# A two-block transformer kernel: the first stage rebuilt, four stalls of TensorE reordered, and every SBUF tile moved to a multiple of 512 bytes

## The chip, the cores and the metric

The kernel is one program on one NeuronCore of a Trainium2 chip. The metric is the device time of one execution in microseconds. TensorE (PE) multiplies, VectorE (DVE), ScalarE (ACT) and GpSimd (POOL) do the element-wise work, and SyncE (SP) issues nearly all transfers. All data are fp32 in memory; a product is made of three fp32r products of "high" and "low" parts.

## What is computed

Two transformer blocks on x of 512 tokens x 1024 features. Only what the change touches is shown:

```python
def rmsnorm(x, g):
    y = x32 * lax.rsqrt(jnp.mean(jnp.square(x32), axis=-1, keepdims=True) + EPS)
    return (y * g).astype(x.dtype)

# block 1
h = rmsnorm(x, norm_mix_g)
q, k, v, xr, gr, g_attn, g_rnn = split(h @ w_in)          # 8 heads of 128 columns each in q, k, v
attn_out = diff_attention(rmsnorm(q), rmsnorm(k), v, rel_bias, lam)
r = sigmoid(conv(xr) @ w_a + b_a); i = sigmoid(conv(xr) @ w_x + b_x)
a = exp(-8 * r * softplus(-lru_lambda));  hidden = scan(a, sqrt(1 - a*a) * i * conv(xr)) * gelu(gr)
x = x + (sigmoid(g_attn) * (attn_out @ w_proj_attn) + sigmoid(g_rnn) * (hidden @ w_proj_rnn)) @ w_out
x = x + square(relu(rmsnorm(x) @ w_up)) @ w_down
# block 2: short convolution, forgetting attention, window attention, a merge of the three with gates,
# cross attention to a memory of 256 tokens, a gated feed-forward layer, a last rmsnorm
```

## The kernel before

Activations are kept transposed, features on the partitions and the 512 tokens along the free axis. A matrix product goes by **units**: one unit is 128 output columns over all of its input, 8 tiles of 128 x 128 weights, 24 matmuls of 128 x 512. For each unit SP loads the weights into one of four slots of RAW (L417), GpSimd cuts them into WH (L597) and WL (L600) after a tiny operation on `gate` (L596), TensorE makes hi x hi, lo x hi and hi x lo into the slot's PSUM bank (L630, L632, L634), and VectorE takes the bank (L1540 and others), mostly times RSTD. The input is HH and HL, the two parts of x times the norm's gain; RSTD, the reciprocal root of the mean square of each token, is applied when a bank is taken, so it isn't needed before that. The list PHASES gives the order of the units; each engine has its own program, and semaphores order them. A unit may start when its weights are cut (`unit_cut`), and the bank's last contents are taken (`taken`).

**First stage.** SP loads the gain, both halves of x, 17 small rows of parameters, three units of weights and ten small tables. TensorE transposes x into two banks in turn (L671), ScalarE copies each into X (L1104), makes HH (L1063) and the square (L1065), VectorE makes HL (L1453) from X and HH and adds the squares into ACC0 (L1458). Between them VectorE takes the transposed parameters and the rows of the bias table (BROW, L1524). Then ones x ACC0 gives the sums (L661), ScalarE the root (L1069), VectorE the reciprocal over 128 x 512 (L1463). TensorE runs the three units of head 0; VectorE takes q and k, then computes softplus(-lru_lambda) by a chain of 24 dependent operations on 128 x 8 (L1591 to L1603), and only then scales q and k (L1549), cuts them, takes v and the attention's constants (L1612). Head 0's scores (L748) wait for all this.

**Attention, 8 heads.** `attend` weaves the 72 matmuls of the next head's three units into the 8 score groups, the transposes (L714) and the value products (L725) of this head, by a `share`. At a head's end a root (L1074, L1075) scales the output (L1641), which is cut into AO (L1645); only after that VectorE begins the next head's row maxima (L1572).

**Recurrent stage, 8 rounds.** Each is `rnn_gates(n)` (L825 to L827), which needs the cut convolution XCH, XCL of VectorE (L1667), and four units. **Merge.** `merge1` has two units a round, one from HH, one from the recurrent output RO, all eight tiles of which the first round waits for. Block 2's merge starts with YC (L928), the convolution's output, and YF.

**Layout.** Tiles lie one behind the other in the order of their `sb(...)` calls; `push` and `pop` reuse memory.

Of the kernel before, what the change touches and what calls it, by code (L numbers as in the profile page):

```python
# [173 lines left out]
def program(nc, x, out, w, causal_rows, window_rows):  # L174

    units = Units()
    with ExitStack() as top:
# [11 lines left out]
        class Sems(dict):  # L189
# [10 lines left out]
            "vector_step": ["tab_masked", "gain_taken", "par_taken", "brow_rows", "decay_abs", "lam_dots", "lam_row", "lam_taken",  # L200
# [3 lines left out]
            "tensor_step": ["gain_done", "par_done", "brow_done", "lam_done", "forget_placed", "mem_stat"],  # L204
# [10 lines left out]
        def norm_event(tag, kind, n):  # L215


            k = int(tag[1]) - 1
# [20 lines left out]
        SUM, NMAX, RS = sb("SUM", [P, 8]), sb("NMAX", [P, 8]), sb("RS", [P, 8])  # L239
        column, n = {}, 0  # L240
# [20 lines left out]

        SQ1, ACC1, STD1 = sb("SQ1", [P, 2, S]), sb("ACC1", [P, S]), sb("STD1", [P, S])

# [5 lines left out]
        SQ0 = sb("SQ0", [P, 2, S])  # L269
        ACC0, STD0 = sb("ACC0", [P, S]), sb("STD0", [P, S])  # L270
        VROWS = sb("VROWS", [P, 2, P])
        ONEHOT = sb("ONEHOT", [BUCKETS + 1, BIAS1_W + BIAS2_W])
        TAB = sb("TAB", [BUCKETS + 1, 2, HEADS])
        BROW = sb("BROW", [HEADS, BIAS1_W + BIAS2_W])
# [3 lines left out]
        LOGT = sb("LOGT", [P, 8, 8])  # L278
# [8 lines left out]
        def attention_memory(tag, parts, cols):  # L287
# [12 lines left out]
            if tag == "a":  # L300
# [9 lines left out]
        XR = sb("XR", [P, S + 3])  # L310
# [4 lines left out]
        MG = sb("MG", [P, DC, S])  # L315
        GA, SG, GT, G2 = SQ1[:, 0, :], SQ1[:, 1, :], ACC1, STD1
# [20 lines left out]
        push()  # L337
        FLEFT = sb("FLEFT", [P, S], F32R)
        FRIGHT = ACC1[:]
        FROW = sb("FROW", [P, 2, S], F32R)  # L340
        pop()
        CB, CC, CV = SQ1[:, 0, :], SQ1[:, 1, :], ACC1[:]
        ZP = sb("ZP", [P, S + 2])
# [32 lines left out]
        ACC, STD, SQS = ({tag: first if tag == "n1" else later for tag in GAIN}  # L376
                         for first, later in ((ACC0, ACC1), (STD0, STD1), (SQ0, SQ1)))

# [31 lines left out]
        def _(sp):  # L410
# [15 lines left out]
            for half in range(2):  # L426
# [21 lines left out]
            for j in range(3):  # L448
                load("qkv", 0, j, cols(w["w_in"], D * j))
            sp.dma_start(ONEHOT[:, 0:BIAS1_W], causal_rows).then_inc(S_["tab_landed"], 16)  # L450
            sp.dma_start(ONEHOT[:, BIAS1_W:], window_rows).then_inc(S_["tab_landed"], 16)
            sp.dma_start(TAB[0:BUCKETS, 0, :], w["rel_bias"]).then_inc(S_["tab_landed"], 16)
            sp.dma_start(TAB[0:BUCKETS, 1, :], w["rel_bias_2"]).then_inc(S_["tab_landed"], 16)
            for k, name in enumerate(("lambda_q1", "lambda_k1", "lambda_q2", "lambda_k2")):
                sp.dma_start(LAM[:, k, :], w[name].rearrange("(o c) -> o c", o=1)).then_inc(S_["lam_landed"], 16)
            sp.dma_start(small[0:HEADS, FBIAS:FBIAS + 1], w["forget_bias_2"].rearrange("(p o) -> p o", o=1)
                         ).then_inc(S_["lam_landed"], 16)
            sp.dma_start(SROW[:, 0:8], w["sink_2"].rearrange("(o c) -> o c", o=1)).then_inc(S_["lam_landed"], 16)

# [5 lines left out]
            for h in range(1, HEADS):  # L465
# [92 lines left out]
        def _(pool):  # L558
            nc.gpsimd.memset(ident[:], 0.0).then_inc(once("ident_clear")[0], 1)
# [1583 lines left out]
```

## Time and profile before

| | us |
|---|---|
| median of 3 runs (lowest, highest) | 2112.77 (2111.72, 2116.9) |
| the profiled execution: its own time | 2114.88 |
| its span, first to last instruction | 2113.1 |
| TensorE busy in it | 1979.3 |
| until the first score of head 0 | 58.54 |
| one attention head in the steady state | 31.40 |
| recurrent stage, from 318.0 to 503.5 | 185.5 |

The span is what the rows are counted in. Busy times of TensorE overlap (a 128 x 512 matmul is shown as 0.39 us, and the next begins 0.23 us after it), so idle time is read from the waits and the starts, not from the busy share.

### The profile page before, as it was taken

Reading aid. Unit: us, or ns where it says so; the run is one execution under the profiler, and the core shown is the slowest. Engines: PE = TensorE matmul, PEld = TensorE weight load, DVE = VectorE, ACT = ScalarE, POOL = GpSimd, SP = SyncE. Lnnn points to the kernel's source line nnn. Section 1 sums busy time; section 2 is a strip of 40 time slices with the busy share of each in tenths; the row PEclk is TensorE's granted clock in tenths of the full one; section 3 lists DMA queues with packets and bytes.
Section 4 is the critical chain, followed back from the end, with each engine's and each line's share of the span. In section 5 each row is a group of like instructions: output and inputs, shape, how many; then the busy total and the mean of one; then the engine's idle time right before and its main releaser. Section 6 shows DMA issues by size and latency. Waiting matters only on the chain.

```text
span 2113.1 us, 23477 instructions
## 1 busy us (share of the span) xinstructions
PE 1979.3 (94%) x9015; PEld 1608.9 (76%) x9015; DVE 1071.6 (51%) x1522; ACT 501.7 (24%) x1001; POOL 1232.1 (58%) x1014
## 2 busy tenths in 40 slices
PE   6888869999999999999799988999989899999997
PEld 4666658887888888888587777888778778888886
DVE  7666658996364132237765664333455463223134
ACT  4444433432122011022233322101222221001012
POOL 6233327777767676666233433677767567667662
PEclk8999989999999999999899989999999999999999
DMA  5122112333333333333112311333433323333321
GB/s 155 46 68 62 47 33 77 105 94 94 95 95 95 93 97 97 92 100 90 50 51 60 70 55 45 100 92 98 120 100 90 90 82 99 94 95 100 90 85 55
DMA packets 341169, 177.39 MB, mean 84 GB/s; under 512 B 14453, under 2 KB 338203, under 8 KB 341060
## 3 DMA queue, kind: packets, MB, share of 16 engines
q1 hardware_dynamic: 339044, 173.28, 28.4%
q10 hardware_dynamic: 2016, 2.62, 0.6%
q8 instruction: 73, 1.20, 0.2%
q14 instruction: 36, 0.29, 0.0%
HBM read 173.75 MB, written 2.13 MB: 83 GB/s over the span
## 4 chain that ended last, share of the span: by engine, by line
PE 75%; DVE 18%; ACT 3%; issue 3%; DMA 0%; ACTq 0%; DVEq 0%; SPq 0%
PE bank L630 22%; PE bank L634 22%; PE bank L632 22%; PE bank L748 2%; PE bank L725 1%; DVE aPR L1580 1%; PE bank L696 1%; DVE aPR L1582 1%; DVE aPR L1572 1%; PE bank L714 1%; DVE HS L1691 1%; DVE IT L1680 1%; DVE ACC L1685 1%; DVE XC L1661 1%; DVE HS L1690 1%
## 5 line engine op out<-in xcount | busy, mean ns | idle before, releaser
L600 POOL TENSOR_TENSOR WL<-RAW,WH 128x1024 fp32r<-128x1024 f32 (+3 forms) x331 | 814.3, 2460 | 27.6
L630 PE MATMUL bank<-HH,WH 128*128 128x512 f32 x1560 | 623.6, 400 | 2.3 <-DVE HL L1453 2.3
L634 PE MATMUL bank<-HH,WL 128*128 128x512 f32 x1560 | 619.0, 397 | 0.0
L632 PE MATMUL bank<-HL,WH 128*128 128x512 f32 x1560 | 616.2, 395 | 0.0
L596 POOL TENSOR_TENSOR gate<-gate 128x1 f32<-128x1 f32 x331 | 81.6, 246 | 822.0 <-PE bank L634 770.9
L630 PEld LDWEIGHTS bank<-HH,WH 128*128 128x128 f32 x1560 | 296.9, 190 | 67.1 <-issue 6.9
L597 POOL TENSOR_SCALAR WH<-RAW 128x1024 fp32r<-128x1024 f32 (+3 forms) x331 | 343.2, 1037 | 0.9 <-issue 0.2
L632 PEld LDWEIGHTS bank<-HL,WH 128*128 128x128 f32 x1560 | 296.4, 190 | 60.8 <-issue 3.1
L634 PEld LDWEIGHTS bank<-HH,WL 128*128 128x128 f32 x1560 | 295.8, 190 | 60.9 <-issue 1.7
L1731 DVE TENSOR_TENSOR X<-X,bank 128x512 f32<-128x512 f32 x80 | 54.9, 686 | 210.6 <-PE bank L634 210.6
L1453 DVE SCALAR_TENSOR_TENSOR HL<-X,PARAM,HH 128x512 fp32r<-128x512 f32 x40 | 89.1, 2226 | 30.3 <-ACT HH L1063 30.3
L630 PE MATMUL bank<-UH,WH 128*128 128x512 f32 x256 | 101.5, 397 | 0.0
L634 PE MATMUL bank<-UH,WL 128*128 128x512 f32 x256 | 101.2, 395 | 0.0
L632 PE MATMUL bank<-UL,WH 128*128 128x512 f32 x256 | 101.2, 395 | 0.0
L1235 ACT ACTIVATE SU<-TU 128x512 f32<-128x512 f32 x32 | 20.3, 636 | 263.5 <-DVE TU L1750 263.4
L1750 DVE SCALAR_TENSOR_TENSOR TU<-bank,RSTD 128x512 f32<-128x512 f32 x32 | 22.1, 692 | 115.5 <-PE bank L634 115.5
L630 PE MATMUL bank<-FFH,WH 128*128 128x512 f32 x176 | 70.3, 399 | 0.6 <-DVE FFL L2067 0.6
L632 PE MATMUL bank<-FFL,WH 128*128 128x512 f32 x176 | 69.6, 395 | 0.0
L634 PE MATMUL bank<-FFH,WL 128*128 128x512 f32 x176 | 69.6, 395 | 0.0
L1540 DVE TENSOR_TENSOR GA<-bank,RSTD 128x512 f32<-128x512 f32 x24 | 16.6, 692 | 102.8 <-PE bank L634 102.8
L1063 ACT ACTIVATE HH<-X,PARAM 128x512 fp32r<-128x512 f32 x40 | 28.9, 723 | 128.5 <-DVE X L1731 128.5
L630 PEld LDWEIGHTS bank<-UH,WH 128*128 128x128 f32 x256 | 48.1, 188 | 12.8 <-issue 1.4
(399 smaller groups left out, 3210.1 us busy)
## 6 DMA issues: line engine op xcount, KB each, us to landing
RAW<-in_w_in SPq DMA_DIRECT2D x107, 512.0 KB, 3.7
RAW<-in_w_up SPq DMA_DIRECT2D x32, 512.0 KB, 4.0
RAW<-in_w_down SPq DMA_DIRECT2D x32, 512.0 KB, 3.9
RAW<-in_w_ffn_gate SPq DMA_DIRECT2D x22, 512.0 KB, 3.7
RAW<-in_w_ffn_up SPq DMA_DIRECT2D x22, 512.0 KB, 3.8
RAW<-in_w_xkv SPq DMA_DIRECT2D x16, 512.0 KB, 3.8
RAW<-in_w_ffn_down SPq DMA_DIRECT2D x16, 512.0 KB, 3.5
RAW<-in_w_proj_attn SPq DMA_DIRECT2D x8, 512.0 KB, 3.9
```

What stands on the lines that cost most here:

```text
L596: nc.gpsimd.tensor_tensor(gate[:, 1:2], gate[:, 0:1], gate[:, 0:1], ALU.add)
L597: nc.gpsimd.tensor_scalar(WH[:, s, 0:k, :], RAW[:, s, 0:k, :], 1.0, 1.0, ALU.mult, ALU.mult).then_inc(S_[f"hi_made{s}"], 1)
L600: nc.gpsimd.tensor_tensor(WL[:, s, 0:k, :], RAW[:, s, 0:k, :], WH[:, s, 0:k, :].bitcast(F32), ALU.subtract).then_inc(S_[f"unit_cut{s}"], 1)
L630: mm(psum[s][:, 0:n], WH[:, s, k, :], hi(k), start=(k == 0), stop=False)
L632: mm(psum[s][:, 0:n], WH[:, s, k, :], lo(k), start=False, stop=False)
L634: last = mm(psum[s][:, 0:n], WL[:, s, k, :], hi(k), start=False, stop=(k == tiles - 1))
L696: mm(STAT[:], lhs, rhs, start=True, stop=True).then_inc(S_[tag + "_stat"], 1)
L748: last = mm(bank, M[q][:, part, i * P:(i + 1) * P], M[k][:, 2, k0:k1], start=(q == "QH" and k == "QH"), stop=(q == "QL" and not add_bias), ...
L1063: A(HH[:, bass.ds(e, 1), :], x_e, ACT.Copy, scale=par(GAIN[tag], e)).then_inc(norm_event(tag, "hh", 0)[0], 1)
L1453: V.scalar_tensor_tensor(HL[:, bass.ds(e, 1), :], X[:, bass.ds(e, 1), :], par(GAIN[tag], e), HH[:, bass.ds(e, 1), :].bitcast(F32), ALU.mul ...
L1731: take(name, it, j, lambda bank: V.tensor_tensor(x_e, x_e, bank[:].unsqueeze(1), ALU.add))
L1750: take("mlp", g, j, lambda bank: V.scalar_tensor_tensor(TU[:, j % 2, :], bank[:], 0.0, RSTD[:], ALU.max, ALU.mult))
```

## The change

- **Loads.** SP loads weights and x in turn: unit 0, first half of x, unit 1, second half, unit 2, then the rows of parameters, and the three units of head 1. The ten small tables and vectors go to ScalarE's queue.
- **x.** Transposes go to four banks. ScalarE makes HH and VectorE HL straight from the bank (one operand in PSUM); VectorE also copies the bank into X, for the last four tiles after all of HL. The sums of squares are made by ScalarE over the tokens (four squares of 128 x 1024 with a running sum, 128 x 1 each); root and reciprocal are on 128 x 4; four diagonal blocks (DIAG) and one matmul with ones spread them into RSTD.
- **Order.** TensorE weaves the transposes, q's and k's products, runs 9 matmuls of v, then the statistic, the bias rows, the rest of v, the parameters, and then the 24 matmuls of head 1's q before head 0's attention; head 0's `share` weaves in the 48 that are left.
- **Decay chain.** The 24 operations are made 5 at a time in heads 1 to 5, between the take of v and the wait for the root.
- **Waits.** `rnn_gates(0)` is run after the next two units; `merge1` waits for RO tile by tile; the merge of block 2 starts with YF and waits for YC tile by tile; `f_out_taken` 9 is asked only before YS.
- **Tiles.** pad_low (96 elements) ahead of X, LOGT and pad_small (16) into the small tiles, XR to the end of its group, ZP (514 wide) replaced by CZ, which lies in STD1, with the taps of the convolution written as shifted ranges; FROW, FLEFT and FRIGHT move to the place of SQ1, ACC1 and STD1.

```diff
@@ layout
+        sb("pad_low", [P, 96])
         X = sb("X", [P, DC, S])
...
         SUM, NMAX, RS = sb("SUM", [P, 8]), sb("NMAX", [P, 8]), sb("RS", [P, 8])
+        LOGT = sb("LOGT", [P, 8, 8])
+        sb("pad_small", [P, 16])
...
+        push()
+        FROW, FLEFT = sb("FROW", [P, 2, S], F32R), sb("FLEFT", [P, S], F32R)
+        pop()
         SQ1, ACC1, STD1 = sb("SQ1", [P, 2, S]), sb("ACC1", [P, S]), sb("STD1", [P, S])
+        FRIGHT = STD1[:]
...
-        XR = sb("XR", [P, S + 3])
         XC = sb("XC", [P, S])
...
         MG = sb("MG", [P, DC, S])
+        XR = sb("XR", [P, S + 3])
...
-        ZP = sb("ZP", [P, S + 2])
...
+        XBANK = [WORK[0], WORK[1], psum[2], psum[3]]
+        X_LATE = (6, 7, 4, 5)
@@ sync
+            load("qkv", 0, 0, cols(w["w_in"], 0))
+            load_x(0)
+            load("qkv", 0, 1, cols(w["w_in"], D))
+            load_x(1)
+            load("qkv", 0, 2, cols(w["w_in"], D * 2))
...
             for j in range(3):
-                load("qkv", 0, j, cols(w["w_in"], D * j))
...
+                load("qkv", 1, j, cols(w["w_in"], P + D * j))
             sp.wait_ge(*once("brow_rows"))
             sp.dma_start(scr, BROW[:]).then_inc(S_["brow_stored"], 16)
@@ gpsimd
-            clear_queries("a", M1, M1["OR"][:])
...
                 cut(name, it, j)
+                if (name, it, j) == ("qkv", 0, 2):
+                    clear_queries("a", M1, M1["OR"][:])
@@ tensor
+            def x_transposed(e):
...
+                if e >= 4:
+                    pe.wait_ge(S_["n1_x"], e - 3)
                 for t in range(NB):
-                    last = nc.tensor.transpose(WORK[e % 2][:, t * P:(t + 1) * P], XTOK[:, t, e * P:(e + 1) * P],
+                    last = nc.tensor.transpose(XBANK[e % 4][:, t * P:(t + 1) * P], XTOK[:, t, e * P:(e + 1) * P],
                                                ident[:])
...
+            for e in range(4):
+                x_transposed(e)
+            queries0, keys0 = from_h("qkv", 0, 0, cut_of("n1")), from_h("qkv", 0, 1)
+            for e in range(DC):
+                run(queries0, 3)
+                if e < 4:
+                    x_transposed(e + 4)
+                if e >= 3:
+                    run(keys0, 3)
+            run(keys0)
+            pe.wait_ge(S_["n1_x"], 5)
+            values0 = from_h("qkv", 0, 2)
+            run(values0, 9)
+            pe.wait_ge(S_["n1_diag"], NB)
+            mm(STAT[:], ones[:], DIAG[:], start=True, stop=True).then_inc(norm_event("n1", "stat", 0)[0], 1)
+            bias_rows()
+            run(values0)
+            parameters()
             pe.wait_ge(*norm_event("n1", "std", 1))
...
+            steps0 = chain(*[from_h("qkv", 1, j) for j in range(3)])
             for side in range(2):
-                run(values0, 9)
+                run(steps0, 6)
                 qk_stat1(0, 0, side)
-            run(values0)
+            run(steps0, 6)
...
+            run(steps0, 6)
             pe.wait_ge(*once("lam_taken"))
+            pe.wait_ge(*once("brow_rows"))
 
             def head1(h, last):
+                if h == 0:
+                    steps, share = steps0, (3, 8, 8, 2)
...
             for n in range(DC):
-                rnn_gates(n)
+                if n:
+                    rnn_gates(n)
...
                 if n == 0:
+                    rnn_gates(0)
...
+                run(from_pair("merge1", e, 1, RO, cut_pair("ro_hi", "ro_lo") if e == 0 else None))
...
-            pe.wait_ge(S_["yc_lo"], 4)
-            pe.wait_ge(S_["f_out_taken"], 9)
+            pe.wait_ge(S_["f_out_taken"], 5)
...
-                for k in range(8):
+                for k in (4, 5, 6, 7, 0, 1, 2, 3):
@@ scalar
+            for e in range(DC):
+                act.wait_ge(S_["xt_done"], e + 1)
+                A(HH[:, e, :], XBANK[e % 4][:], ACT.Copy, scale=par(GAIN["n1"], e)
+                  ).then_inc(norm_event("n1", "hh", 0)[0], 1)
...
+                if e in (3, 4, 5, 7):
+                    token_squares({3: 0, 4: 1, 5: 2, 7: 3}[e])
+            act.wait_ge(S_["n1_ssq"], NB)
+            A(SSQ[:], SSQ[:], ACT.Sqrt, bias=EPSC[:], scale=1.0 / D).then_inc(S_["n1_root"], 1)
@@ vector
             for e in range(DC):
-                norm_chunk("n1", e, e % 2)
...
+                V.scalar_tensor_tensor(HL[:, e, :], XBANK[e % 4][:], par(GAIN["n1"], e), HH[:, e, :].bitcast(F32),
+                                       ALU.mult, ALU.subtract).then_inc(norm_event("n1", "hl", 0)[0], 1)
+                if e < 4:
+                    x_copy(e)
+            for e in X_LATE:
+                x_copy(e)
...
+            own.link(V.reciprocal(SSQ[:], SSQ[:]))
+            for t in range(NB):
+                V.tensor_scalar(DIAG[:, t * P:(t + 1) * P], ident[:], SSQ[:, t:t + 1], None, ALU.mult
+                                ).then_inc(S_["n1_diag"], 1)
+            dve.wait_ge(*norm_event("n1", "stat", 1))
+            V.tensor_copy(RSTD[:], STAT[:]).then_inc(norm_event("n1", "std", 0)[0], 1)
...
             take_qk1(0, 0)
+            take_qk1(0, 1)
+            bias_rows()
+            parameters()
...
                     take("qkv", h + 1, 2, scaled(M1["VR"][:]))
+                for _step in range(5 if 0 < h else 0):
+                    next(decays, None)
```

## Rows read from the trace of the kernel before

**Rows 1.** The page's totals by engine.

```profile
PE 1979.3 (94%) x9015; PEld 1608.9 (76%) x9015; DVE 1071.6 (51%) x1522; ACT 501.7 (24%) x1001; POOL 1232.1 (58%) x1014
```

**Rows 2.** Table of stretches: start:end, length, busy us of each engine, clock, DMA.

```profile
0.00:58.54 58.54, 34.75 (x121) 23.52 (x122) 47.40 (x84) 24.45 (x39) 31.84 (x37) 0.80 0.52 148
58.54:90.06 31.52, 28.97 (x129) 22.82 (x129) 19.04 (x42) 13.24 (x31) 8.38 (x8) 0.93 0.14 43
90.06:121.46 31.40, 27.58 (x130) 20.93 (x129) 20.87 (x44) 14.97 (x34) 11.09 (x10) 1.00 0.20 59
318.00:503.50 185.50, 180.78 (x787) 147.56 (x787) 168.09 (x135) 70.39 (x94) 145.35 (x117) 1.00 0.33 95
```

**Rows 3.** The waits of PE over the span: total us, times, longest.

```profile
PE bank L748 <- DVE small L1612: 11.7, 1, 11.7
...
PE bank L825 <- DVE XCL L1667: 9.4, 1, 9.4
...
PE bank L928 <- DVE YCL L1922: 1.8, 1, 1.8
```

**Rows 4.** Timeline, 0 to 58 us: start, us, engine, line, what.

```profile
6.33 1.94 PE L671 MATMUL bank<-ident,XTOK 128*128 128x128 f32 x8 [6.33 <-DMA XTOK<-in_x]
...
10.04 0.71 ACT L1063 ACTIVATE HH<-X,PARAM 128x512 fp32r<-128x512 f32 x1
...
10.87 0.75 DVE L1453 SCALAR_TENSOR_TENSOR HL<-X,PARAM,HH 128x512 fp32r<-128x512 f32 x1 [2.12 <-ACT HH L1063]
...
13.13 0.68 POOL L596 TENSOR_TENSOR gate<-gate 128x1 f32<-128x1 f32 x1 [7.27 <-DMA RAW<-in_w_in]
...
15.28 2.83 DVE L1458 TENSOR_TENSOR ACC<-ACC,SQ 128x512 f32<-128x512 f32 x1
...
32.77 1.02 PE L661 MATMUL bank<-ACC,ones 128*128 128x512 f32 x2
...
34.62 3.35 DVE L1463 RECIPROCAL RSTD<-STD 128x512 f32<-128x512 f32 x1 [1.58 <-ACT STD L1069]
...
42.13 2.21 DVE L1593 TENSOR_TENSOR LOGT<-LOGT 128x8 f32<-128x8 f32 x1
...
44.38 0.17 DVE L1594 TENSOR_TENSOR LOGT<-LOGT 128x8 f32<-128x8 f32 x1
```

**Rows 5.** What the DMA engines moved, 0 to 60 us in 40 slices of 1.5 us.

```profile
GB/s 0 15 393 400 399 238 202 271 312 272 82 3 0 0 0 0 0 0 0 22 46 210 244 333 291 303 266 77 302 41 178 172 57 288 5 233 117 0 0 0
```

**Rows 6.** Timeline, 482 us: a PSUM-sourced VectorE instruction beside a GpSimd one.

```profile
482.29 2.72 POOL L600 TENSOR_TENSOR WL<-RAW,WH 128x1024 fp32r<-128x1024 f32 x1
...
482.67 0.68 DVE L1698 SCALAR_TENSOR_TENSOR MG<-SQ,bank 128x512 f32<-128x512 f32 x1
```

**Rows 7.** Timeline, 120 to 127 us: the seam between attention heads 1 and 2.

```profile
120.73 1.05 POOL L597 TENSOR_SCALAR WH<-RAW 128x1024 fp32r<-128x1024 f32 x1
...
121.86 2.39 POOL L600 TENSOR_TENSOR WL<-RAW,WH 128x1024 fp32r<-128x1024 f32 x1
...
123.45 1.35 DVE L1641 SCALAR_TENSOR_TENSOR aOR<-aOR,small,aRQ 128x512 f32<-128x512 f32 x1 [2.29 <-ACT aRQ L1075]
...
126.53 0.39 PE L748 MATMUL bank<-aQH 128*128 128x256 f32 x1 [1.08 <-DVE NMAX L1572]
```

**Rows 8.** Timeline of the recurrent stage: two waits of DVE, and PE's at its end.

```profile
324.26 0.69 DVE L1656 TENSOR_TENSOR XR<-bank,RSTD 128x512 f32<-128x512 f32 x1 [1.55 <-PE bank L634]
...
347.63 0.69 DVE L1656 TENSOR_TENSOR XR<-bank,RSTD 128x512 f32<-128x512 f32 x1 [1.71 <-PE bank L634]
...
503.52 0.77 PE L630 MATMUL bank<-ROH,WH 128*128 128x512 f32 x1 [4.75 <-issue]
```

**Rows 9.** PE's timeline: first matmuls of 384 on HH/HL, of 192 on FFH/FFL, and the next.

```profile
1865.14 0.39 PE L630 MATMUL bank<-HH,WH 128*128 128x512 f32 x1
...
1952.23 0.39 PE L630 MATMUL bank<-FFH,WH 128*128 128x512 f32 x1
...
1997.20 0.39 PE L630 MATMUL bank<-HH,WH 128*128 128x512 f32 x1
```

More of the change, by code:

```diff
@@ L375, in program @@
                 "n5": "ffn_norm_g_2", "n6": "final_norm_g_2"}
-        ACC, STD, SQS = ({tag: first if tag == "n1" else later for tag in GAIN}
-                         for first, later in ((ACC0, ACC1), (STD0, STD1), (SQ0, SQ1)))
+        ACC, STD, SQS = ({tag: tile for tag in GAIN if tag != "n1"} for tile in (ACC1, STD1, SQ1))
+        XBANK = [WORK[0], WORK[1], psum[2], psum[3]]
+        X_LATE = (6, 7, 4, 5)
         scr = nc.dram_tensor("bias_rows", [HEADS, BIAS1_W + BIAS2_W], F32).ap()
@@ L425, in _, with load_x @@
             sp.dma_start(VROWS[0:r, 0, :], w[name].rearrange("(r c) -> r c", c=P)).then_inc(S_["gain_landed"], 16)
-            for half in range(2):
+            def load_x(half):
                 sp.dma_start(XTOK[:, :, half * S:(half + 1) * S],
@@ L464, in _ @@
                 sp.dma_start(BIAS1[:, h, :], toeplitz_of(h, 0)).then_inc(S_[f"bias_landed{h}"], 16)
-            for h in range(1, HEADS):
+            for h in range(2, HEADS):
                 for j in range(3):
@@ L558, in _ @@
         def _(pool):
+            for s in range(SLOTS):
+                pool.sem_inc(S_[f"unit_cut{s}"], 1)
+                pool.sem_inc(S_[f"hi_made{s}"], 1)
             nc.gpsimd.memset(ident[:], 0.0).then_inc(once("ident_clear")[0], 1)
@@ L688, in _, with parameters @@
-            mm(psum[2][0:8, 128:512], TAB[:, 1, :], ONEHOT[:, 640:1024], start=True, stop=True
-               ).then_inc(once("brow_done")[0], 1)
+            def parameters():
+                pe.wait_ge(S_["rows_landed"], 16 * N_ROW_LOADS)
+                pe.wait_ge(*once("gain_taken"))
+                na, nb = sum(r for _, r in ROWS_A), sum(r for _, r in ROWS_B) + 2
+                nc.tensor.transpose(OUTB[:, 0:na], VROWS[0:na, 0, :], ident[0:na, 0:na])
+                nc.tensor.transpose(OUTB[:, 96:96 + nb], VROWS[0:nb, 1, :], ident[0:nb, 0:nb]
+                                    ).then_inc(once("par_done")[0], 1)
@@ L795, in _ @@
             pe.wait_ge(S_["lam_landed"], 96)
-            mm(psum[3][:, 0:16], ones[0:1, :], SROW[0:1, 0:16], start=True, stop=True).then_inc(once("lam_done")[0], 1)
+            pe.wait_ge(*once("par_taken"))
+            mm(OUTB[:, 160:176], ones[0:1, :], SROW[0:1, 0:16], start=True, stop=True).then_inc(once("lam_done")[0], 1)
+            run(steps0, 6)
             pe.wait_ge(*once("lam_taken"))
+            pe.wait_ge(*once("brow_rows"))
             def head1(h, last):
-                steps = chain(from_h("first", 0, 0), from_h("first", 0, 1)) if last else \
-                    chain(*[from_h("qkv", h + 1, j) for j in range(3)])
-                attend("a", M1, KIND1, h, steps, (2, 8, 8, 3) if last else (5, 10, 10, 2),
+                if h == 0:
+                    steps, share = steps0, (3, 8, 8, 2)
+                elif last:
+                    steps, share = chain(from_h("first", 0, 0), from_h("first", 0, 1)), (2, 8, 8, 3)
+                else:
+                    steps, share = chain(*[from_h("qkv", h + 1, j) for j in range(3)]), (5, 10, 10, 2)
+                attend("a", M1, KIND1, h, steps, share,
@@ L843, in _ @@
                     run(from_h("rnn", n, 4))
-            for e in range(DC):
-                run(from_h("merge1", e, 0))
-                if e == 0:
-                    pe.wait_ge(S_["ro_hi"], DC)
-                    pe.wait_ge(S_["ro_lo"], DC)
-                run(from_pair("merge1", e, 1, RO))
             def cut_pair(hi, lo, base=0):
@@ L1143, in _ @@
             qk_hi1(0, 1)
+            act.wait_ge(*once("decay_abs"))
+            A(LOGT[:, 1, :], LOGT[:, 0, :], ACT.Exp, scale=-1.0).then_inc(once("decay_exp")[0], 1)
             def head1(h, last):
@@ L1905, in conv2 @@
                 if n == 3:
-                    take(*conv_unit(h, last, 2), scaled(ZP[:, 2:]))
+                    take(*conv_unit(h, last, 2), scaled(CZ))
                 if n == 4:
```

196 lines of the change are left out of this document (91 added, 105 removed).

## The prediction

> **What bounds the kernel now.** I read the page's totals first: TensorE is busy 94% of the span [rows 1], so a change is worth what it takes from TensorE's idle time or from the spacing of its matmuls. The list of its waits says where it idles [rows 3]: 11.7 us before head 0's first score, 9.4 us before the first `rnn_gates`, 1.8 us before the merge of block 2. A wait of 4.75 us before the first product from RO is seen in the timeline alone [rows 8]. The table of stretches [rows 2] shows the largest loss: head 0's attention begins at 58.54 us, with 72 product matmuls done, which take 3 x 5.44 = 16.3 us at the later spacing [rows 9], and TensorE's clock is 0.80 of full on average there. VectorE is busy 47.4 of these 58.5 us: the first stage is bound by VectorE, and in part by its collisions with GpSimd. A head later in the run lasts 31.4 us, TensorE and VectorE waiting for each other.
>
> **First stage, to head 0's first score.** The load of unit 0 is put ahead of x, unit 1 between its halves. The halves of x moved at 393 to 400 GB/s and weights at 202 to 312 [rows 5], from 3.0 us on; 2.1 MB at 398 and 1.05 MB at 290 are 8.9 us, so the second half lands at about 12.4; I take 13. Unit 0 of before landed at 13.13 [rows 4] with 2.5 MB moved; 3 MB pro rata give 15.8 as the late end, 12 is the early one. The first half, 6.33 before, comes some 2 us later, behind transposes that have four banks and don't wait.
> From there ScalarE sets the pace: four HH of 0.71 and three squares over 1024 columns, which no row shows; twice the 0.71 of a 512-wide pass is 1.42 each. 13 + 2.8 + 4.3 = 20.1. The last HL is 0.75 more: 20.9. Four copies into X, priced as a PSUM-sourced 0.68 [rows 6], give 23.6. HL reads one operand from PSUM now. Such an instruction took 0.68 us while a GpSimd cut of 2.72 ran [rows 6], whereas one with both operands in SBUF was held for 2.83 [rows 4]; so I charge HL and copies no collision.
> Then come two products of 64 numbers and four diagonal blocks in SBUF, with GpSimd cutting units 2 and 3 all the while. Six such instructions cost 0.17 us free or 2.21 held [rows 4], hence 1.0 to 13.3; of these two neighbours one was held and one not, so I take the mean 1.19 x 6 = 7.1, and 30.7 us for the matmul with ones. The former reciprocal over 128 x 512 (3.35) and the eight additions are gone.
> Behind it on TensorE's queue: the statistic 1.0 (one pair of row L661), three bias-row products, priced as two such pairs 2.0, 15 matmuls of v 3.4, the parameters 0.4, 6 matmuls 1.4, q's statistic 1.0, 6 more 1.4, k's statistic 1.0: 11.6. Then root 1.4 (two passes of 0.71), scaling 0.75 (as HL), cut 0.7 and 0.7, the take of v 0.7, constants 0.4: 4.6. Head 0 begins at 30.7 + 16.2 = 46.9, say 47. TensorE's own work bounds it from below: four units of 5.44 after 13 us, with eight us of transposes, statistics and rows, is 43. From above, the late x and the held six give 56. The gain is 11.5 us, from 15.5 to 2.5.
> The bias rows now reach SP some 3 us after RSTD, and their store and load have 13 us until 47. Head 1's loads stand ahead of them on SP's queue and wait at most for units 0 and 1 to be cut, by then long done.
>
> **Head 0.** 24 of its 72 matmuls are done, 5.4 us. Head 0 took 31.52 at a clock of 0.93, which is 2 us of half speed. TensorE's last idle stretch shrinks from 11.7 to 3 or 4 us, so I count these 2. Of the 5.4 only part comes back, since TensorE idles already 3.8 us a head (31.4 less 27.6 busy) [rows 2] for VectorE; bounds 0 and 5.4, and nearly the middle, 2.5. Together 4.5.
>
> **Decay chain.** In heads 1 to 5, five operations stand on VectorE in a pause of 2.29 us before L1641 [rows 7]. Free they take 5 x 0.2 and hide. But GpSimd's cut of 1.05 and 2.39 lies over that pause. Two pass beside the first part, the third is held until 124.25, two more and L1641 (0.75, no longer held) end at 125.45 instead of 124.80. VectorE's next maxima, and TensorE's second score pair (idle 1.08 there), are queued behind it, so it is on the path: 0.65 x 5 = 3.3, say 3.5 us lost. Bounds: 0, and 24 x 2.0 = 48 if each were held in a cut of its own.
>
> **Recurrent stage.** Two units (10.9 us) run in the 9.4 us pause and TensorE leads by as much. VectorE, though, isn't sooner: its first round hangs on `rnn_gates(0)`, whose operands come when they came. It is busy 168.1 of 185.5 us [rows 2], and waited for TensorE in the first two rounds only, 1.55 and 1.71 [rows 8]. These 3.3 us are the floor of what the stage ends sooner, the whole 9.4 the ceiling; VectorE's idle time is mostly short waits for ScalarE, so I stay near the floor with 4.5. TensorE's lead becomes idle time at RO's last tile. There the wait by tiles helps: 21 of 24 matmuls, 4.9 us at 0.234, are done before it. Sum 9.4, from 5 to 14.
>
> **Block 2's merge.** YF's 12 matmuls cover the wait for YC: 1.8 us. The convolution's two shifted ranges and the missing border cost nothing that TensorE waits for.
>
> **Tiles.** 384 matmuls on HH and HL take 1952.23 - 1865.14 = 87.09 us, 0.2268 each; 192 on FFH and FFL take 44.97, 0.2342 each, at the same clock with no waits [rows 9]. It is 5.44 against 5.62 a unit. From the tiles' order and sizes, if each is rounded up to 32 bytes and the four one-element constants come first, HH and HL start 128 bytes past a multiple of 512, and all tiles after the small ones 320 or 352 past it. After the change all are at 0. I take the start of the moving tile as the cause of the two spacings, and the better one as what the others get. 98 units of U, FF, AO in `out1`, RO, MGC, XO and Y are outside the VectorE-bound stages: 98 x 0.178 = 17.4 us; the memory's half-wide matmuls 0.6: 18. Nothing shows where 0 stands, so the bounds are wide: nothing gained, or a further step of 0.178 a unit, for 147 units of HH and HL as well, 17.4 + 26.2 = 43.6 more.
> The Trainium skill (TensorE: Matmul & The Clock Gate, Back-to-back issue gap) gives 215.7 ns for isolated matmuls of 512 columns at the full clock, and no word on alignment; no row here is that short. By it, some 5,900 matmuls would give about 80 us in place of 18.
>
> **Sum.** 2113.1 - 11.5 - 4.5 + 3.5 - 9.4 - 1.8 - 18 = 2071.4. The span stands 0.3 us over the median of the runs, and the profiled execution's own time is 1.8 over it: I predict 2071 us for the median.
>
> **Rivals.**
> *No gain by alignment*: the two spacings come from something else (HH lies lowest in memory; the others are all above it). For it: place and alignment can't be told apart in this trace. 2071 + 18 = 2089.
> *A second step*: HH's spacing falls too. For it: HH isn't at a multiple of 512 either. 2071 - 44 = 2027.
> *The first stage doesn't gain*: VectorE's six instructions and the late x fill what was freed, head 0 begins near 58. For it: GpSimd's queue is full from 14 us on, where it idled before. 2071 + 16 = 2087.
> The rule of the skill (SBUF, Who interferes with whom) is that VectorE instructions with two SBUF inputs, or in a two-port mode, and GpSimd's exclude each other for a whole instruction. The trace agrees [rows 4, 6], 2.83 against 0.68; by it the diagonal blocks are held and HL isn't, as the sum has it.
> *Slower*: 0 is the bad place. If HH's unit grows by 0.178, 147 units cost 26.2, and nothing is won on the others: 2071 + 18 + 26 = 2115, no change. Two such steps make 2141. It decides from a spacing of HH of about 0.236 us. Against it: of the two starts seen, the one with more factors of two is the faster.
>
> **How the numbers follow.** Forecast 42%; no gain by alignment 25%; second step 14%; first stage without gain 9%; bad place 7%, of which more than half slower; the rest is several at once. The range reaches from the second step to past the two cases near 2088: 2025 to 2100. The forecast's own range is 2060 to 2081. Faster by over 0.3% (6.3 us, about what a measurement of this kernel can tell from no change) has 0.91, within it 0.05, slower 0.04.
>
> **What would show it.** Head 0's first score at 47 (43 to 56); the next head's 27 us later; heads 1 to 5 at 32.0, head 6 under 31.4; no wait of 9.4 but a longer one at RO's last tile, before only three matmuls; units of U and FF at 5.44 us. I am wrong if x's second half lands past 16, if the decay operations take over 2 us each, or if HH's own spacing moves.

## The result, and the profile after

The changed kernel takes 2086.34 us, median of 4 runs (2084.80 to 2087.51); the kernel before took 2112.57 beside it. The ratio is 0.9871 (95% interval 0.9854 to 0.9888), a gain of 26 us against a forecast of 42 (2071). It lies in the range of 2025 to 2100, and on the side that had 0.91, but outside the forecast's own range of 2060 to 2081, and four of the five gains came out smaller. The profiled execution has a span of 2083.0 us and a time of its own of 2084.80; it is the fastest of its four, and that of the kernel before was 2.3 us over its median, so the two profiles differ by 30 us where the medians differ by 26.

The page's totals (busy us, share of the span, instructions), which answer to [rows 1]:

```profile
PE 1956.0 (94%) x9015; PEld 1605.8 (77%) x9015; DVE 1070.7 (51%) x1525; ACT 495.2 (24%) x992; POOL 1232.8 (59%) x1014
```

The table of stretches, cut at the same events as [rows 2] (columns as there: PE, PEld, DVE, ACT, POOL, TensorE's granted clock, DMA):

```profile
0.00:50.21 50.21, 34.28 (x146) 25.50 (x146) 30.82 (x64) 18.13 (x30) 34.11 (x40) 0.98 0.57 174
50.21:80.69 30.48, 24.93 (x105) 19.41 (x105) 18.85 (x42) 13.53 (x31) 6.76 (x6) 0.87 0.14 42
80.69:111.53 30.84, 27.65 (x131) 20.93 (x129) 20.55 (x45) 14.97 (x34) 9.65 (x9) 1.00 0.20 60
309.28:493.70 184.42, 173.05 (x746) 141.97 (x744) 166.16 (x133) 70.15 (x93) 142.61 (x114) 0.95 0.32 93
```

TensorE's waits over the span, which answer to [rows 3]:

```profile
PE bank L749 <- DVE small L1678: 7.7, 1, 7.7
PE bank L629 <- DVE SQ L1599: 7.4, 1, 7.4
...
PE bank L670 <- DMA XTOK<-in_x: 5.7, 1, 5.7
...
PE bank L850 <- DVE XCL L1735: 3.9, 1, 3.9
```

The wait before head 0 fell from 11.7 to 7.7 us, that for YC is gone, and that for XCL fell from 9.4 to 3.9; but one of 7.4 us is new. The stretches between landmarks of TensorE's timeline, in the profiled executions (the third column is an experiment, told below, that has the layout alone):

| from, to | before | layout alone | changed | changed less before | forecast |
|---|---|---|---|---|---|
| start, head 0's first score | 58.54 | 58.16 | 50.21 | -8.3 | -11.5 |
| to head 1's | 31.52 | 31.82 | 30.48 | -1.0 | -4.5 |
| to head 7's | 187.75 | 187.92 | 190.38 | +2.6 | +3.5 |
| to the first matmul on UH | 399.73 | 396.58 | 393.05 | -6.7 | -9.4 and some 3 of alignment |
| to the first on fQH | 350.04 | 345.49 | 345.48 | -4.6 | alignment |
| to the first on MGCH | 470.21 | 469.27 | 464.77 | -5.4 | -1.8 and alignment |
| to the first on XKH | 78.61 | 78.17 | 78.32 | -0.3 | alignment |
| to the first on XOH | 110.74 | 111.00 | 108.02 | -2.7 | none |
| to the end of the span | 425.96 | 421.59 | 422.29 | -3.7 | alignment |

Read down, the column gives -30.1, the difference of the spans. The layout alone accounts for 13.1 of it; what the rest of the change brings, 17.0, is won ahead of UH (10.4), from fQH to MGCH, the stretch with block 2's merge in it (4.5), and in cross attention (3.0), with small losses elsewhere.

### The profile page after: what moved, and what is told of

Same layout as the page of the kernel before. It is cut to its first block, busy times and chain, and to the rows that moved or that the text cites. A ratio compares the mean times of both kernels' runs of the same rounds, so it can differ in the third digit from the quotient of the medians.

```text
span 2083.0 us, 23467 instructions
## 1 busy us (share of the span) xinstructions
PE 1956.0 (94%) x9015; PEld 1605.8 (77%) x9015; DVE 1070.7 (51%) x1525; ACT 495.2 (24%) x992; POOL 1232.8 (59%) x1014
## 4 chain that ended last, share of the span: by engine, by line
PE 76%; DVE 19%; ACT 3%; issue 2%; DMA 0%; ACTq 0%; SPq 0%; DVEq 0%
PE bank L629 22%; PE bank L633 22%; PE bank L631 22%; PE bank L749 2%; PE bank L726 1%; DVE aPR L1639 1%; DVE IT L1748 1%; DVE aPR L1641 1%; DVE XC L1729 1%; DVE HS L1758 1%; DVE HS L1759 1%; PE bank L715 1%; PE bank L697 1%; DVE aPR L1631 1%; DVE ACC L1753 1%
## 5 line engine op out<-in xcount | busy, mean ns | idle before, releaser
L1497 DVE SCALAR_TENSOR_TENSOR HL<-X,PARAM,HH 128x512 fp32r<-128x512 f32 x32 | 79.8, 2493 | 27.7 <-ACT HH L1090 27.7
L629 PEld LDWEIGHTS bank<-UH,WH 128*128 128x128 f32 x256 | 48.1, 188 | 11.7 <-issue 1.9
L1599 DVE TENSOR_TENSOR FGA<-bank,RSTD 128x512 f32<-128x512 f32 x22 | 15.2, 692 | 79.7 <-PE bank L633 79.7
```

Of the source, the lines that this page charges most:

```text
L629: mm(psum[s][:, 0:n], WH[:, s, k, :], hi(k), start=(k == 0), stop=False)
L1497: V.scalar_tensor_tensor(HL[:, bass.ds(e, 1), :], X[:, bass.ds(e, 1), :], par(GAIN[tag], e), HH[:, bass.ds(e, 1), :].bitcast(F32), ALU.mul ...
L1599: return lambda bank: V.tensor_tensor(dst, bank[:], RSTD[:], ALU.mult)
```

## Experiments: what the layout is worth, and why

In the sessions of the experiments the kernel before took 2116.8 to 2118.1 us, 4.2 to 5.5 us more than beside the change. So times of one session are compared as they are, and times of different sessions by their ratios to the kernel before. A spacing is the mean from start to start of neighbouring matmuls on the same tile, longer gaps (240 ns and more; 260 for FF at 384 bytes) left out, and for HH and HL the attention stages too.

**The layout alone.** The kernel before with the new places of the tiles, with CZ and its shifted ranges for ZP, and nothing else of the change:

```diff
+        sb("pad_low", [P, 96])
         X = sb("X", [P, DC, S])
...
+        sb("pad_small", [P, 80])
...
-        XR = sb("XR", [P, S + 3])
         XC = sb("XC", [P, S])
...
         MG = sb("MG", [P, DC, S])
+        XR = sb("XR", [P, S + 3])
```

> The kernel before with the layout of the change alone: a pad of 96 elements ahead of X and of 80 behind the small tiles, XR last in its group, FROW, FLEFT and FRIGHT in the place of SQ1, ACC1 and STD1, ZP replaced by CZ with the shifted ranges of the convolution. If the start of the moving tile sets the spacing: the units of U, FF, AO, XO, MGC and RO fall from 233.3 to 226.8 ns a matmul, HH and HL stay, and the kernel takes 2113 - 18 = 2095 us (98 units of 24 matmuls, 6.4 ns each, are 15; units of AO and of Y in bound stages may bring up to 3 more). If the spacing came from another part of the change (the order, the clock): no spacing moves and the time is 2113.

Measured: 2100.81 us, ratio 0.9924 (0.9908 to 0.9940), 13 to 19 us gained. The spacing fell from 233.3 to between 226.8 and 227.3 ns for U (756 gaps), FF, AO, XO, MGC and RO; HH and HL went from 227.06 to 226.80. So the layout does it, without the new order. The memory's half-wide matmuls went the other way, from 116.9 to 119.8 ns (365 gaps under 130 ns; the 117.8 of the expectations leaves out some 75 gaps of 113 and 114 ns). Of block 2's 1.8 us wait for YC nothing changed here.

**Which place is bad?** Two shifts of all tiles of the changed kernel at once, one edit each:

```diff
-        sb("pad_low", [P, 96])
+        sb("pad_low", [P, 80])
```

> The changed kernel with pad_low of 80 elements in place of 96, so that every large tile, HH and HL among them, starts 448 bytes past a multiple of 512, which is 64 past one of 128. If the start decides: HH and HL go to 233.3 ns too, as the other tiles do, and with some 240 units of 24 matmuls at 6.4 ns more the kernel takes up to 37 us more than the changed one, about 2120. If the place in memory decides (the lowest tiles fast, those above slow): HH and HL stay at 226.8 and the others return to 233.3: 2086 + 15 = 2101. If neither: 2086.

```diff
-        sb("pad_low", [P, 96])
```

> The changed kernel without pad_low: every large tile starts 128 bytes past a multiple of 512, where HH and HL stood before. If multiples of 128 are enough, all units stay at 226.8 ns and the time at 2086 us. If 0 is better than 128 for the other tiles (or for the half-wide matmuls on the memory, 119.9 ns now and 117.8 before), it shows here: MEM at 117.8 and 2 x 128 x 3 x 2 ns = 1.5 us gained, or lost elsewhere.

Measured: 2087.43 and 2089.06 us, ratios 0.9859 (0.9841 to 0.9877) and 0.9866 (0.9851 to 0.9881): no difference to the changed kernel. Every spacing of 128x512 matmuls stayed at 226.6 to 227.4 ns, the memory's at 119.8. Both readings that I had, a bad start of the moving tile and a bad region of memory, fall: starts of 0, 128 and 448 past a multiple of 512 are equally good. What all these versions have in common, and the kernel before had not, is that the moving tile and the weights WH and WL stand at the same place past a multiple of 512. Before, U and the others stood at 320, the weights at 128, 192 apart; HH and HL at 128, 0 apart.

**Start or distance?** First everything at 320, the place of U before:

```diff
-        sb("pad_low", [P, 96])
+        sb("pad_low", [P, 48])
```

> The changed kernel with pad_low of 48 elements: every large tile, the weights WH and WL too, starts 320 bytes past a multiple of 512, which is where U, FF, AO, XO, MGC and RO stood before, at 233.3 ns. Theory A, the start of the moving tile itself (320 is a bad place, while 0, 128 and 448 are good): all units, those of HH and HL too, go to 233.3 ns and the kernel takes 2086 + 35 = about 2120 us. Theory B, what counts is the distance from the start of the weights' tile to that of the moving tile, past a multiple of 512 (before: 192 for U and the others, 0 for HH; in all the versions of the change so far 0): nothing moves, 226.8 ns and 2086 to 2088 us.

Then U at 448, a good place in the first shift, with the weights at 256:

```diff
-        sb("pad_low", [P, 96])
+        sb("pad_low", [P, 32])
...
-        sb("pad_small", [P, 16])
+        sb("pad_small", [P, 64])
```

> The changed kernel with pad_low 32 and pad_small 64 elements: HH, HL, WH, WL at 256 past a multiple of 512, U, FF, AO, XO, MGC, RO and the attention's tiles at 448, which was a good place when all stood there. Theory A (the moving tile's own start): 226.8 ns and 2087 us. Theory B (the distance to the weights, here 192 as in the kernel before): HH and HL stay at 226.8, the others go to 233.3 ns, the memory's half-wide matmuls from 119.9 back to 117.8, and the kernel takes about 2086 + 15 to 18 = 2103 us.

Measured: 2087.96 us with every spacing at 226.6 to 227.3 ns, and 2102.69 us (the two ran on the same chip, ratios 0.9864, 0.9849 to 0.9878, and 0.9932, 0.9917 to 0.9947) with U, FF, AO, XO and RO at 233.3, HH and HL at 227.05 and the memory at 116.8. Theory B stands, 14.7 us for the 192 bytes.

**The weights moved alone.** The sharpest form: all moving tiles stay where they are in the changed kernel, at 0.

```diff
+        sb("pad_w", [P, 80])
         WH, WL = sb("WH", [P, SLOTS, DC, P], F32R), sb("WL", [P, SLOTS, DC, P], F32R)
+        sb("pad_behind", [P, 48])
```

> The changed kernel with only WH and WL moved (80 elements ahead of them, 48 behind, so that every other tile stays at a multiple of 512): weights at 320 past one, every moving tile at 0, which is 192 apart as U and the others were from the weights before. If the distance to the weights decides, HH and HL, which were at 226.8 ns in every version so far, go to 233.3 ns with all the others; outside the attention and recurrent stages there are 215 units of 24 matmuls, 215 x 24 x 6.5 ns = 33.5 us, less 0.8 for the memory's half-wide matmuls (117.8 again): about 2119 us, no faster than the kernel before. If it is the distance to another tile (X, RAW, the banks) or a mere place: HH and HL stay at 226.8 ns, and the time at 2087.

Measured: 2123.60 us, slower than the kernel before (ratio 1.0033, 1.0023 to 1.0043). HH and HL, never slow until here, are at 233.35 ns over 3228 gaps, U at 233.33, the memory at 115.5. TensorE's timeline shows it without any averaging. The changed kernel's first matmuls of a stretch of 384 on HH and HL, of 192 on FFH and FFL, and of the next on HH, as in [rows 9]:

```profile
1836.06 0.39 PE L629 MATMUL bank<-HH,WH 128*128 128x512 f32 x1
...
1923.10 0.39 PE L629 MATMUL bank<-FFH,WH 128*128 128x512 f32 x1
...
1966.98 0.39 PE L629 MATMUL bank<-HH,WH 128*128 128x512 f32 x1
```

and the same three with the weights moved:

```profile
1869.03 0.39 PE L631 MATMUL bank<-HH,WH 128*128 128x512 f32 x1
...
1958.63 0.39 PE L631 MATMUL bank<-FFH,WH 128*128 128x512 f32 x1
...
2003.60 0.39 PE L631 MATMUL bank<-HH,WH 128*128 128x512 f32 x1
```

The duration printed is 0.39 in all of them; only the starts tell. HH's 384 take 87.04 us in the first and 89.60 in the second (87.09 before); FF's 192 take 43.88 and 44.97 (44.97 before).

**Which distances?** Pads ahead of single groups, so that one run has seven distances:

```diff
+        sb("pad_ao", [P, 80])
         AO = sb("AOH", [P, DC, S], F32R), sb("AOL", [P, DC, S], F32R)
...
+        sb("pad_ro", [P, 80])
         RO = sb("ROH", [P, DC, S], F32R), sb("ROL", [P, DC, S], F32R)
...
+        sb("pad_u", [P, 16])
         UH, UL = sb("UH", [P, DC, S], F32R), sb("UL", [P, DC, S], F32R)
```

and 112 ahead of MGCH, 64 ahead of MEMH, 96 ahead of FFH.

> The changed kernel with a pad ahead of single groups, so that the moving tiles stand at different distances from WH and WL, past a multiple of 512 bytes: HH and HL 0, U 64, RO 128, XO and the memory 256, AO 320, FF 384, MGC 448 (192 was measured: 233.3 ns). If every distance but 0 costs: all but HH and HL are at 233.3 ns. If it is 192 and its mirror 320 alone, or the half of them, their spacings show which. The memory's half-wide matmuls at 256: 117.8 as at 192, or 119.9 as at 0. The time is 2086 plus 6.4 ns for each matmul of a slow group, at most 2103 us.

Measured: 2093.40 us, ratio 0.9894 (0.9878 to 0.9911). The place of the moving tile less that of the weights, past a multiple of 512, against the mean spacing:

| bytes apart | 0 | 64 | 128 | 192 | 256 | 320 | 384 | 448 |
|---|---|---|---|---|---|---|---|---|
| tile | HH | U | RO | U (other run) | XO | AO | FF | MGC |
| ns | 227.1 | 231.0 | 233.1 | 233.3 | 226.7 | 231.3 | 232.8 | 233.4 |

The two halves repeat each other: what counts is the distance past a multiple of 256. That each distance has another tile here does no harm: at 0 all these tiles stood at 226.6 to 227.4, at 192 all at 233.3 or 233.4. But at 64 and 320 the mean hides two levels. U's four long stretches (169 gaps each) stand at 233.3, 229.0, 233.3 and 228.9, AO in the recurrent stage at 229.4 to 229.7 and later at 233.3. So something besides the distance counts there, and what it is stays open. The memory's matmuls of 256 columns at 256 apart are at 119.8 ns, as at 0.

## Experiments: the order

**GpSimd kept off the cuts before head 0.** In the changed kernel the time from the matmul with ones to head 0's first score was 22.8 us, 16.2 in the forecast. The changed kernel's timeline from 40 us on, VectorE and GpSimd:

```profile
40.50 0.19 POOL L593 TENSOR_TENSOR gate<-gate 128x1 f32<-128x1 f32 x1 [8.54 <-DMA RAW<-in_w_in]
...
40.65 1.05 POOL L594 TENSOR_SCALAR WH<-RAW 128x1024 fp32r<-128x1024 f32 x1
40.67 1.56 DVE L1608 SCALAR_TENSOR_TENSOR aQN<-aQN,PARAM,aRQ 128x512 f32<-128x512 f32 x1 [1.88 <-ACT aRQ L1102]
...
41.78 2.67 POOL L597 TENSOR_TENSOR WL<-RAW,WH 128x1024 fp32r<-128x1024 f32 x1
42.16 4.43 DVE L1621 TENSOR_TENSOR aQL<-aQN,aQH 64x512 fp32r<-64x512 f32 x2
...
46.14 2.65 POOL L597 TENSOR_TENSOR WL<-RAW,WH 128x1024 fp32r<-128x1024 f32 x1
46.62 2.72 DVE L1615 TENSOR_TENSOR aQL<-aQN,aQH 128x512 fp32r<-128x512 f32 x1
```

GpSimd had been idle for 8.5 us, because head 2's loads stand behind the bias rows on SP's queue, and its first two cuts fall on VectorE's last four instructions before head 0. The edit:

```diff
             for name, it, j in units.order:
...
+                if (name, it, j) == ("qkv", 2, 0):
+                    pool.wait_ge(S_["a_qk_lo"], 3)
                 cut(name, it, j)
```

> The changed kernel with one wait more: GpSimd cuts the first unit of head 2 only when VectorE has made head 0's low parts of q and k (they took 4.43 and 2.72 us beside the two cuts). If that collision is what kept the first score at 50.21 us: the three take 0.75, 0.75 and 0.75 (k's scaling 0.75 in place of 1.56 too), the first score comes at 45 to 46, TensorE's idle stretch before it falls from 7.7 to 3 or 4 us, its clock falls less or not, and 3 to 6 us are gained if the cuts do not collide with head 0's maxima instead. Rival: the same collision moves into head 0 (its units are cut later, beside the takes and the softmax), the first score comes sooner, head 0 lasts longer by as much, and the kernel stays at 2086.

Measured: 2078.48 us, ratio 0.9816 (0.9802 to 0.9831), against 2087.43 and 2089.06 for the two shifted kernels beside it that have the changed order: 9 to 11 us. Its timeline at the same place:

```profile
40.23 0.75 DVE L1610 SCALAR_TENSOR_TENSOR aQN<-aQN,PARAM,aRQ 128x512 f32<-128x512 f32 x1 [1.88 <-ACT aRQ L1104]
40.90 1.39 DVE L1623 TENSOR_TENSOR aQL<-aQN,aQH 64x512 fp32r<-64x512 f32 x2
...
42.33 0.69 DVE L1617 TENSOR_TENSOR aQL<-aQN,aQH 128x512 fp32r<-128x512 f32 x1
...
43.10 0.19 POOL L593 TENSOR_TENSOR gate<-gate 128x1 f32<-128x1 f32 x1 [10.70 <-DVE aQL L1617]
...
43.88 0.33 PE L751 MATMUL bank<-aQH 128*128 128x128 f32 x1 [1.76 <-DVE small L1680]
```

The four instructions took 2.83 us in place of 8.71, 5.88 less, and the time from the matmul with ones to the first score was 16.92 in place of 22.80, 5.88 less as well: the collision is all of the difference. The first score came at 43.88, earlier than I had hoped for, TensorE's wait before it fell from 7.67 to 1.76 us, and head 0 took 29.34 at a clock of 0.94, not 30.48 at 0.87. The rival, that the collision would move into head 0, did not come. The Trainium skill (SBUF — State Buffer, Who interferes with whom) says that a VectorE instruction with two SBUF inputs and a GpSimd one that reads SBUF exclude each other for a whole instruction; these rows agree, 1.39 against 4.43 us for the same pair.

**The decay chain.** On top of that edit, the chain leaves the heads for VectorE's two pauses before head 0 (and ScalarE's exponential for it stands ahead of its first root):

```diff
             for side in range(2):
+                for _step in range((14, 10)[side]):
+                    next(decays, None)
                 norm_qk1(0, side, side)
...
-                for _step in range(5 if 0 < h else 0):
-                    next(decays, None)
```

> The changed kernel with GpSimd waiting as in the run of that edit (2078.5 us), and the decay chain taken out of heads 1 to 5: its 24 operations stand in VectorE's two pauses ahead of head 0 instead (2.64 us before q is scaled, 1.88 before k), 14 and 10, while GpSimd waits. If the chain in the heads cost what their lengths say: heads 2 to 5 fall from 32.1 back to 31.4 us, 4 x 0.7 = 2.8 us, the first score stays within 0.3 us of 43.9 (24 x 0.17 = 4.1 in 4.5 us of pauses), and the kernel takes 2075.5. If the heads lengthened for another reason (the alignment, the loads): they stay at 32.1 and nothing is gained.

Measured: 2077.69 us, ratio 0.9816 (0.9801 to 0.9830): the time is the same, though the heads did what was expected. Head 0's first score came at 43.52, heads 2 to 5 took 31.45 us in place of 32.1, and head 7 began 3.6 us sooner. Head 7 up to the first matmul on XCH then gave 2.8 of these back. Two kernels of one order show what that stretch can do. The table of stretches from head 7's first score to XCH, of the changed kernel with all tiles at 448:

```profile
270.11:308.11 38.00, 32.88 (x150) 26.00 (x149) 20.96 (x47) 13.19 (x31) 10.29 (x8) 0.96 0.11 32
```

with all tiles at 128:

```profile
268.16:309.01 40.85, 35.75 (x150) 28.48 (x149) 21.03 (x47) 13.29 (x31) 10.25 (x8) 0.87 0.10 30
```

and of this run:

```profile
261.60:303.10 41.50, 35.93 (x150) 28.39 (x149) 21.15 (x47) 13.34 (x31) 10.26 (x8) 0.88 0.10 30
```

The same 150 matmuls and the same work of VectorE last 38.0 us where TensorE's granted clock is 0.96 and 40.9 where it is 0.87 (the share is of 2.4 GHz; in part of the time 1.2 is granted). Versions of one order fall on either side, so one profile cannot tell whether the chain's 3 us are always lost there; the medians say that they were not won.

**rnn_gates(0) first again.** 

```diff
             for n in range(DC):
-                if n:
-                    rnn_gates(n)
+                rnn_gates(n)
...
                 if n == 0:
-                    rnn_gates(0)
```

> The changed kernel with rnn_gates(0) put back ahead of the two units. If the order is worth something: TensorE idles some 9 us before its first matmul on XCH again, and the first matmul on UH comes later by up to 4 us (the forecast's 4.5 less what the wait at RO gave back). If VectorE sets the stage's end in either order (its last operation on ROL stood 223.6 us behind the first score of head 7 before, 225.5 in the changed kernel): the 9 us come back, the 7.4 us wait near the stage's end is gone, ROL's last operation doesn't come later, and the time stays within 1 us or even falls.

Measured: 2080.98 us, ratio 0.9839 (0.9821 to 0.9857), against 2087.96 and 0.9864 (0.9849 to 0.9878) for the order of the change beside it. The four runs spread from 2077.08 to 2086.53 and the intervals overlap, so this pair alone doesn't show a gain; the pair told last, in one session, does. In the trace, the first matmul on UH stood 389.89 us behind head 7's first score, not 393.05. What the order of the change does, in its timeline:

```profile
307.13 0.69 DVE L1735 TENSOR_TENSOR XCL<-XC,XCH 128x512 fp32r<-128x512 f32 x1 [0.70 <-ACT XCH L1219]
...
309.28 0.39 PE L850 MATMUL bank<-XCH,WH 128*128 128x512 f32 x1
...
325.60 0.76 PE L850 MATMUL bank<-XCH,WH 128*128 128x512 f32 x1 [3.93 <-DVE XCL L1735]
...
335.94 0.77 PE L629 MATMUL bank<-HH,WH 128*128 128x512 f32 x1 [7.44 <-DVE SQ L1599]
```

XCL is ready at 307.82, but TensorE is still in the second unit until 309.28, and VectorE waits for the gates 1.5 us longer. Within two rounds TensorE idles 3.93 and 7.44 us, 11.4 in place of the 9.4 that were saved, and its clock from 320 to 360 us is 0.79. With the gates first it idles 9.41 us once and then not at all up to the merge, in its timeline:

```profile
303.67 0.76 PE L850 MATMUL bank<-XCH,WH 128*128 128x512 f32 x1 [9.41 <-DVE XCL L1733]
```

and in its table of stretches, from XCH to ROH:

```profile
303.67:486.30 182.63, 182.63 (x793) 150.63 (x794) 164.75 (x134) 70.98 (x94) 141.89 (x114) 0.98 0.33 94
```

From XCH to ROH both profiles with the gates first take 182.5 and 182.6 us; the seven with the order of the change and the wait by tiles, those with 192 bytes left aside, take 184.3 to 184.7.

**RO at once.** The first round of `merge1` waits for all of RO again:

```diff
+                if e == 0:
+                    pe.wait_ge(S_["ro_hi"], DC)
+                    pe.wait_ge(S_["ro_lo"], DC)
-                run(from_pair("merge1", e, 1, RO, cut_pair("ro_hi", "ro_lo") if e == 0 else None))
+                run(from_pair("merge1", e, 1, RO))
```

> The changed kernel with the first round of merge1 waiting for all eight tiles of RO before its first matmul on them. If the wait by tiles is what the stage gained: the 21 matmuls that ran ahead of the last tile stand behind it, 21 x 0.227 = 4.8 us, and the kernel takes 2091. If something else bounds the seam (the slots that VectorE takes late, the 7.4 us wait): nothing changes by more than 1 us.

Measured: 2090.66 us, ratio 0.9878 (0.9863 to 0.9894), 2.7 more than the kernel beside it (2087.96); the intervals overlap, so the trace has to decide. From XCH to the first matmul on RO it took 189.66 us, not 184.42, and from there to UH 1.1 more, with the wait in plain sight:

```profile
502.07 0.76 PE L629 MATMUL bank<-ROH,WH 128*128 128x512 f32 x1 [4.88 <-issue]
```

The wait by tiles is worth 5.2 + 1.1 = 6.3 us in these two profiles.

**All that helped.** GpSimd's wait, the chain in the pauses and the gates first, the edits above in one kernel:

> The same with rnn_gates(0) ahead of the two units, as before the change. That order alone gave the first matmul on UH 389.9 us behind head 7's first score in place of 393.05. If the gain is the order's: 3 us less than without it, about 2072.5 us, the fastest so far. If it was chance of that run: no difference to the kernel without it.

Measured: 2074.13 us, ratio 0.9799 (0.9785 to 0.9814). It is 3.6 us below the same without the gates first, and no run of one reaches the other (2073.58 to 2075.36 against 2076.55 to 2079.02). By the ratios it is some 15 us below the change, and the fastest version.

## Why the prediction was right, and where it was off

The direction and most of the mechanism were right, and the size was not: 26 us for 42. That 2086 lies in the range owes something to luck. The range was wide because two rivals stand at 2087 and 2089, and the result stands beside them, though neither happened: the tiles brought what the layout brings, and the first stage gained 8.3 us. Gains that nobody had forecast, 2.7 us in cross attention and some 2 ahead of block 2's merge, fill a part of what was missing.

- **First stage** (-11.5 forecast, -8.3 found). Until 27.4 us all went better than forecast: x's second half landed by 12.65, the first square over 1024 columns took 1.05 and 0.19 in place of 1.42, the matmul with ones stood at 27.41 against 30.7. (It stood behind v's nine matmuls then and not behind the diagonal blocks, which were done at 26.09. And 3.0 + 8.9 is 11.9, not 12.4, for the landing of x's second half; by the slices of rows 5, 3.2 MB and not 2.5 had moved by 13.13.) The step that failed is the sum behind it, 11.6 + 4.6 us with every VectorE instruction at its free price, though it put GpSimd "cutting units 2 and 3 all the while" beside the earlier ones only. Its next cuts, behind late loads, held q's and k's. With GpSimd kept off, the stretch took 16.92 us, near the 16.2 of the sum, so the rest of the sum came out. In five other profiles of the same order up to head 0 (all at 448, 128 and 320, the distances, the gates first) the score stood at 46.4 to 47.7, which is the forecast's 47; in three more (192 apart, the weights moved, RO at once) at 49.8 to 50.2. So the size of this collision changes from version to version: the four instructions took 5.6 to 6.6 us in the five, 8.6 in the three, 8.7 in the changed kernel. The five reach 47 by two errors that cancel, 3 to 4 us too much before the matmul with ones and 3.5 to 4.5 too little behind it.
- **Head 0** (-4.5, -1.0). The 2 us of half speed were counted as won if TensorE's idle stretch shrank to 3 or 4. It was 7.7, and the clock 0.87. With the idle stretch at 1.76 the head took 29.34 at a clock of 0.94, against 31.52 at 0.93: at nearly one clock the 24 matmuls done beforehand are worth 2.2 in this pair of profiles, close to the 2.5 counted. It is the 2 us of clock that never came.
- **Decay chain** (+3.5, +2.6). The step by step forecast holds: the third operation was held for 2.2 us and L1709 ended 0.7 later. Each of heads 2 to 5 lengthened by 0.7, head 6 by 0.4, head 1 was shorter by 0.6; with the chain out of the heads they take 31.45 again.
- **Recurrent stage** (-9.4, some -3.6 beside the alignment). The wait by tiles is as forecast (6.3 for 4.9). The 4.5 for moved gates has the wrong sign, +3.2. I had written that the gates' operands come when they came; I had not asked whether TensorE would be free when they came. It was 1.5 us late, and the lead became idle time two rounds on; the longer wait forecast at RO's last tile was 0.2. That VectorE bounds the stage was wrong too: with the gates first TensorE waits for nothing in all of it.
- **Block 2's merge** (-1.8). The wait went. The whole stretch gained 5.4, of which the layout has 0.9. Of the other 4.5, 3.8 are ahead of the merge's first matmul (271.27 us from fQH with the layout alone, 267.49 changed): the wait and 2.0 more, at the same other waits of TensorE. Where these 2.0 come from stays open.
- **Tiles** (-18; -13.1 in the profile with the layout alone, 16 by its ratio, 14.7 by putting 192 bytes back). Which units change, and where to, was right, and the mechanism, the start of the tile, was wrong. The term was sized too high by a stretch's own joints: a unit of FF gained 1.09 / 8 = 0.136 us, not 0.178, and 98 x 0.136 is 13.3. The memory lost about 1.1 (384 x 2.9 ns) where 0.6 was to be gained.
- **Not forecast:** cross attention took 2.7 us less at the same waits, at a granted clock of 0.98. The changed kernel's stretch from XKH to XOH in the table of stretches:

```profile
1552.69:1660.71 108.02, 98.19 (x620) 88.29 (x621) 48.84 (x93) 23.68 (x58) 71.28 (x56) 0.98 0.33 98
```

  and that of the kernel before:

```profile
1576.40:1687.14 110.74, 100.78 (x620) 90.00 (x621) 49.28 (x93) 23.72 (x58) 71.33 (x56) 0.95 0.33 95
```

  With the layout alone it is 111.00 at 0.95, with the changed order and the tiles 192 bytes apart 110.54 and 110.86 at 0.95; the ten other profiles of the changed order are all at 108.0 to 108.5. So it takes both, the order and a layout without the 192 bytes. Why the clock differs stays open.
- **Rivals.** "No gain by alignment" and "a second step" fell with the first comparison. "The first stage doesn't gain" didn't happen, though its reason, VectorE held by GpSimd, took 5.9 us of the gain. "A bad place" is real, as the run with the weights moved shows (2123.6 us, for 2115 to 2141 forecast), but it is a distance and the change has none.

## What to carry over

Place the moving tiles and the weights of 128x512 fp32r matmuls at the same offset past a multiple of 256 bytes (256 columns went the other way here), and judge it by the starts of the matmuls, since their printed length does not change. Before work is moved ahead of a wait, ask whether the engine will be back when the operand comes; if not, the time saved returns later with interest. When a first stage is packed tighter, look at what the other user of SBUF does in its last microseconds: one added wait on GpSimd was worth 9 us by the medians, a third of what the whole change had brought.

## What the runs showed of the hardware

- Matmuls of 128x512 in fp32r follow each other at 226.6 to 227.4 ns on average when the moving tile and the weights are 0 or 256 bytes apart past a multiple of 512, and at 231.0 to 233.4 ns at the six other distances measured (single stretches at 64 and 320: 228.9 to 233.3); the start itself (0, 128, 320, 448) does nothing. The Trainium skill (SBUF — State Buffer, Who interferes with whom) lists TensorE's reads of the moving operand and of the weights as two ports, independent of each other; here the spacing depends on where the two tiles stand to each other, by up to 6.6 ns a matmul. By what mechanism, no run shows.
- Matmuls of 128x256 behave the other way: 119.8 ns at 0 and 256 apart, 116.8 and 115.5 at 192.
- TensorE's granted clock differs between kernels of one order, and differences of the size of an edit go with it: head 7 up to XCH takes 2.9 us more at 0.87 than at 0.96. Why one version gets the one and another the other stays open.
